# Row normalisation by columns behind the transposes, a deferred inverse in attention, and new gate order in a two-layer diffusion block

## The reference

```
for layer in (0, 1):
    m_l = split(silu(c) @ w_mod[layer] + b_mod[layer], 6)       # latents
    m_c = split(silu(c_ctx) @ w_mod[layer] + b_mod[layer], 6)   # context
    z = concat(rms(xc) * (1 + m_c[1]) + m_c[0], rms(xl) * (1 + m_l[1]) + m_l[0])
    layer 0: p = z @ w_in; half is mixed by an RWKV-7 scan, half by a gated linear
             recurrence (RG-LRU), both ways in time; y @ w_out
    layer 1: differential attention: softmax(s0) @ v - lam * softmax(s1) @ v, rms, y @ w_o
    x = x + m[2] * y
    h = rms(x) * (1 + m[4]) + m[3]
    x = x + m[5] * peer(h)       # 8 heads x 16 experts per token, gathered from a table
```

## Time and profile before

| | |
|---|---|
| median of 3 runs | 3174.97 us (3174.1 to 3178.06) |
| the profiled execution | 3177.49 us, its span 3175.6 us |
| mean granted clock of TensorE | 0.956 |
| PE busy | 2640.8 us (83%) |
| DVE busy | 2108.9 us (66%) |
| POOL busy | 1077.6 us (34%) |
| ACT busy | 679.6 us (21%) |
| HBM read | 928 MB, mean 293 GB/s |

### The profile page before, as it was taken

The page is one execution under the profiler, slowest core; times in us unless marked ns, Lnnn a source line. Parts: engine busy times, 40 slices in busy tenths (PEclk is TensorE's granted clock), DMA queues, the critical chain, the costliest instruction groups (busy, mean ns, idle before and its releaser), DMA issues. The chain is left out here.

```text
span 3175.6 us, 31187 instructions
## 1 busy us (share of the span) xinstructions
PE 2640.8 (83%) x9164; PEld 1303.7 (41%) x9164; DVE 2108.9 (66%) x4866; ACT 679.6 (21%) x1701; POOL 1077.6 (34%) x927
## 2 busy tenths in 40 slices
PE   4996999996899998787777787776987788887777
PEld 2441888883444443222322232223434444432222
DVE  2236334335567777888888888885575677778887
ACT  1025333331221211111111111112024222111111
POOL 0002233222144444444444444441000243344443
PEclk8997999998999999999999999998998899999999
DMA  5224000005499999999999999997422699999998
GB/s 203 80 100 195 1 1 1 1 1 216 168 400 400 398 405 396 421 421 417 416 421 421 420 413 421 420 420 296 169 69 93 255 419 420 420 419 411 421 421 333
DMA packets 137393, 930.65 MB, mean 293 GB/s; under 512 B 16954, under 2 KB 17978, under 8 KB 32330
## 3 DMA queue, kind: packets, MB, share of 16 engines
q0 software_dynamic: 113664, 822.20, 63.2%
q1 hardware_dynamic: 23636, 107.25, 8.9%
HBM read 928.26 MB, written 1.13 MB: 293 GB/s over the span
## 5 line engine op out<-in xcount | busy, mean ns | idle before, releaser
L1469 PE MATMUL psum<-ring,diag 128*128 128x512 f32 x3072 | 1495.7, 622 | 350.6 <-DVE diag L1588 348.7
L1347 POOL DMA_INDIRECT ring<-in_uv,experts x768 | 914.3, 1191 | 1283.8 <-PE psum L1469 1036.2
L1642 DVE CUSTOM_DVE_ANT_0 ring<-ring,hcur 128x1024 f32<-128x1024 f32 x768 | 941.6, 1226 | 303.6 <-DMA ring<-in_uv,experts 276.0
L1469 PEld LDWEIGHTS psum<-ring,diag 128*128 128x128 f32 x3072 | 558.0, 194 | 1200.1 <-DVE diag L1588 726.0
L1377 ACT ACTIVATE gel<-dots 128x1 f32<-128x1 f32 x768 | 148.6, 201 | 1419.3 <-DVE dots L1642 1418.0
L1588 DVE TENSOR_SCALAR diag<-ident,gel,wcur 128x128 f32<-128x128 f32 x768 | 257.6, 345 | 21.9 <-ACT gel L1377 21.9
L1059 DVE COPY_PREDICATED T<-level,psum 128x512 f32<-128x512 uint32 x80 | 58.6, 733 | 173.8 <-PE psum L824 173.8
L344 PE MATMUL psum<-zT,win_ring 128*128 128x512 f32 x368 | 161.4, 599 | 1.4 <-PEq L90 1.4
L1708 PE MATMUL psum<-wqkv_ring,zT 128*128 128x512 f32 x320 | 139.4, 598 | 1.4 <-PEq L90 1.4
L1448 PE MATMUL psum<-yT,w_q 128*128 128x512 f32 (+1 forms) x256 | 120.3, 572 | 2.6 <-issue 2.6
L344 PEld LDWEIGHTS psum<-zT,win_ring 128*128 128x128 f32 x368 | 70.2, 192 | 87.8 <-issue 87.8
(11 more groups left out here) (368 smaller groups left out, 2702.0 us busy)
## 6 DMA issues: line engine op xcount, KB each, us to landing
wmod<-in_w_mod SPq DMA_DIRECT2D x24, 1024.0 KB, 8.8
w_q<-in_w_q SPq DMA_DIRECT2D x36, 512.0 KB, 7.9
wmod<-in_w_mod POOLq DMA_DIRECT2D x16, 1024.0 KB, 5.5
ring<-in_uv,experts POOLq DMA_INDIRECT x768
wqkv_ring<-in_w_qkv SPq DMA_DIRECT2D x6, 2048.0 KB, 10.7
win_ring<-in_w_in SPq DMA_DIRECT2D x23, 512.0 KB, 3.6
wring<-in_w_mod SPq DMA_DIRECT2D x4, 2048.0 KB, 11.7
bc<-modulation_rows SPq DMA_DIRECT2D x14, 512.0 KB, 13.0
```

Source lines behind the costliest of these rows:

```text
L1347: nc.gpsimd.indirect_dma_start(ring[:, s % RING], None, uv, bass.IndirectOffsetOnAxis(ap=experts[:, n, j:j + 1], axis=0)).then_inc(row_in[ ...
L1469: m = nc.tensor.matmul(ps[:, c], diag[:, j % DIAGS], ring[:, j % RING, D + 512 * c:D + 512 * c + 512], start=(first and j == 0), stop=(las ...
L1642: nc.vector.tensor_tensor_reduce(u, u, hcur[:], 1.0, 0.0, ALU.mult, ALU.add, dots[:, j:j + 1]).then_inc(dot_done, 1)
```

## The change

**Layer 0's normalisation moves into `modulation`.** The weight ring becomes four halves of 1 MB, the same tile that `rglru` uses. While slabs arrive, ACT squares x, DVE multiplies x by the inverse root, PE transposes, ACT copies to zT. The rows of shift and scale are no longer written to DRAM; PE turns them to columns, one per partition, and ACT and DVE apply scale and shift to zT in eight pieces of 128x256 each. On PE the transposes stand ahead of the first modulation matmul.

```diff
+                for t in range(TILES):
+                    nc.scalar.activation(z[:, t], X[:, t], ACT.Square, accum_out=ss[:, t:t + 1]).then_inc(ss_done, 1)
...
+                for g in range(2 * TILES):
+                    act.wait_ge(tr_mm, g + 1)
...
+                act.wait_ge(col_done, 1)
+                shift_scale_act(nc, modcol, 0, zT, lambda k, seg: zT[:, k, seg * SEG:(seg + 1) * SEG], range(0, KD, 2), range(2))
...
+                for i in range(HALVES):
+                    if i >= RING:
+                        sp.wait_ge(part_mm, i - RING + 1)
...
+def columns_of(nc, pe, bank, row, ident, row_done):
+    for n in range(FIRST_CHUNKS):
+        if row_done is not None:
+            pe.wait_ge(row_done, n + 1)
+        for c in range(4 * n, 4 * n + 4):
+            m = nc.tensor.transpose(bank[:, 2 * c:2 * c + 2], row[:, c * P:(c + 1) * P], ident[0:2, 0:2])
+    return m
...
+def shift_scale_act(nc, modcol, layer, zT, source, ks, segs, done=None):
+    for seg in segs:
+        for k in ks:
+            nc.scalar.activation(zT[:, k, seg * SEG:(seg + 1) * SEG], source(k, seg), ACT.Identity,
+                                 scale=modcol[:, layer, 1, k, seg:seg + 1], bias=modcol[:, layer, 0, k, seg:seg + 1])
...
+def keep_busy(nc, bank, ident, rhs, count):
+    for _ in range(count):
+        nc.tensor.matmul(bank, ident, rhs, start=True, stop=True)
```

```diff
+                for t in range(2):
+                    nc.scalar.activation(z[:, t], X[:, t], ACT.Square, accum_out=ss[:, t:t + 1]).then_inc(ss_done, 1)
...
+                for seg in range(2):
+                    act.wait_ge(tr_mm, seg + 1)
+                    shift_scale_act(nc, modcol, 1, zT, source, (0, 1, 4, 5), (seg,))
...
+                    nc.vector.tensor_scalar(z[:, t], X[:, t], ss[:, t:t + 1], None, ALU.mult).then_inc(z_done, 1)
+                    if t == 1:
+                        dve.wait_ge(col_mm, 1)
...
+                keep_busy(nc, ps[:, 0], ident[:], X[:, 0, 0:512], 4)
+                pe.wait_ge(row_in, 16)
+                columns_of(nc, pe, ps[:, 7], row, ident, None).then_inc(col_mm, 1)
```

```diff
-        MOD_AT = lambda u: range(u, u + 1)
+        ROOTS_AT = {3: range(0, 4), 5: range(4, 6), 7: range(6, 8)}
+        SCAN_AT = {4: (0,), 5: (1,), 6: (2,), 7: (3, 4)}
...
-                    if u >= 1:
-                        for n in MOD_AT(u - 1):
-                            mod_groups(n)
-                for n in MOD_AT(7):
-                    mod_groups(n)
+                    if u >= 2:
+                        mod_groups(u - 2)
+                mod_groups(6)
+                mod_groups(7)
                 add_groups(len(LRU_CHUNKS) - 1)
+                keep_busy(nc, ps[:, 0], gw[:, 0], xb[:, 0], 8)
...
-                    if u % 4 == 3:
+                    if u in ROOTS_AT:
                         act.wait_ge(v_done, u + 1)
-                        for q in range(u - 3, u + 1):
+                        for q in ROOTS_AT[u]:
                             nc.scalar.activation(vv[:, q], vv[:, q], ACT.Sqrt).then_inc(m_done, 1)
-                    for n in MOD_AT(u):
...
+                    if u >= 2:
+                        copy_part(u - 2)
+                copy_part(6)
+                copy_part(7)
...
-                    if u >= 4:
-                        scan(u - 4)
-                    if u >= 1:
-                        for n in MOD_AT(u - 1):
-                            mod_row(n)
-                for u in range(4, 8):
+                    for q in SCAN_AT.get(u, ()):
+                        scan(q)
+                    if u >= 3:
+                        mod_row(u - 3)
+                for u in range(5, 8):
                     scan(u)
-                    if u == 4:
-                        for n in MOD_AT(7):
-                            mod_row(n)
+                    mod_row(u)
```

```diff
-                    if g >= 4:
-                        late(g - 4)
+                    if g in (4, 6):
+                        late((g - 4) // 2)
...
-                    nc.scalar.activation(sq[:, u % 2], ps[:, OUT, 0:P], ACT.Square, accum_out=ss[:, u % 2, u // 2:u // 2 + 1]).then_inc(sq_done, 1)
+                    nc.scalar.activation(sq[:, u % 2], ps[:, OUT, 0:P], ACT.Square, scale=inv[:, u % 2, 0:1], accum_out=ss[:, u % 2, u // 2:u // 2 + 1]).then_inc(sq_done, 1)
...
-                    tt(o[:, u % 2, u // 2], ps[:, OUT, 0:P], sub_g[:], ALU.mult).then_inc(o_done, 1)
+                    nc.vector.scalar_tensor_tensor(o[:, u % 2, u // 2], ps[:, OUT, 0:P], inv[:, u % 2, 0:1], sub_g[:], ALU.mult, ALU.mult).then_inc(o_done, 1)
...
-                    step(nc.vector.reciprocal(tot[:, b], tot[:, b]))
-                    step(tt(tot[:, b, 1:2], tot[:, b, 1:2], nlam[:], ALU.mult))
-                    step(nc.vector.tensor_scalar(A[:, b], E[:, b, 0], tot[:, b, 0:1], None, ALU.mult))
-                    nc.vector.scalar_tensor_tensor(A[:, b], E[:, b, 1], tot[:, b, 1:2], A[:, b], ALU.mult, ALU.add).then_inc(a_done, 1)
+                    if u >= 2:
+                        dve.wait_ge(o_done, u - 1)
+                    step(nc.vector.reciprocal(inv[:, b], tot[:, b]))
+                    step(nc.vector.tensor_scalar(inv[:, b, 1:2], inv[:, b, 1:2], tot[:, b, 0:1], nlam[:], ALU.mult, ALU.mult))
+                    nc.vector.scalar_tensor_tensor(A[:, b], E[:, b, 1], inv[:, b, 1:2], E[:, b, 0], ALU.mult, ALU.add).then_inc(a_done, 1)
```

More of the change, by code:

```diff
@@ L254, in _ @@
             def _(sp):
-                for seg in segs:
-                    for i, part in enumerate((shift, scale)):
-                        sp.dma_start(bc[:, seg, i], row_of(mod, layer, seg, part)).then_inc(bc_in, 16)
-                if load_next:
-                    load_next(sp)
+                sp.dma_start(row[:], mod[1, :, 0:2 * D]).then_inc(row_in, 16)
+                load_next(sp)
             @block.scalar
             def _(act):
-                for i, t in enumerate(tiles):
-                    if i >= 2:
-                        act.wait_ge(ss_done, i - 1)
-                    nc.scalar.activation(squares[:, i % 2], X[:, t], ACT.Square, accum_out=ss[:, i:i + 1]).then_inc(ss_done, 1)
+                for t in range(2):
+                    nc.scalar.activation(z[:, t], X[:, t], ACT.Square, accum_out=ss[:, t:t + 1]).then_inc(ss_done, 1)
@@ L267, in _ @@
                 act.wait_ge(mean_done, 1)
                 nc.scalar.activation(ss[:], ss[:], ACT.Sqrt).then_inc(std_done, 1)
-                for g in range(2 * nt):
-                    act.wait_ge(tr_done, g + 1)
-                    i, half = g // 2, 4 * (g % 2)
-                    nc.scalar.activation(hT[:, half:half + 4, i * P:(i + 1) * P],
-                                         ps[:, g % 8].rearrange("p (c t) -> p c t", c=4), ACT.Copy).then_inc(ev_done, 1)
+                act.wait_ge(col_done, 1)
@@ L1848, in values, with late @@
                     m.then_inc(pv_mm, 1)
-                def late(n):
-                    if n >= 2:
-                        pe.wait_ge(late_done, n - 1)
-                    nc.tensor.matmul(ps[0:2, 6 + n % 2], ones[:], mod_acc[:, n], start=True, stop=True).then_inc(late_mm, 1)
+                def late(j):
+                    for g in range(GROUPS):
+                        m = nc.tensor.matmul(ps[32 * g:32 * g + 32, 6 + j], ones[:], mod_acc[:, GROUPS * j + g], start=True, stop=True)
+                    m.then_inc(late_mm, 1)
                 pe.wait_ge(ones_done, 1)
```

199 lines of the change are left out of this document (125 added, 74 removed).

## The result

The changed kernel takes 3153.8 us (median of 4 runs, 3150.7 to 3156.1) where the kernel before, on the same chip, took 3176.5. The ratio is 0.9932 (95% interval 0.9920 to 0.9944): faster, by 17.8 to 25.4 us, that is by less than 1%. The forecast was 3144.5, that is 30.5 us less, with a range of 3138 to 3152; the measured time lies outside it. The profiled execution took 3153.75 us, so it stands at the median and needs no correction.

What follows compares the result with a forecast made beforehand. No engine is busy for the whole span, so it was read by phase: -17.2 + 5.7 - 0.5 - 3.8 - 8.2 - 6.5 = -30.5 us, from a median of 3175.0 to 3144.5, range 3138 to 3152.

Steps and rivals of the forecast that it cites:

- part 2: Gates' stage: the new order makes ACT wait for PE ahead of each Tanh; +5.7 us, bounds -4.5 to +11.
- part 6: Attention: -6.5 us, 6 from transposes, 0.5 from the loop; a ring of waits between ACT and DVE keeps its period 3.46.
- Part 1: Opening: first projection matmul at 46.9 us, 17.2 saved; 21 if the ring of four half slabs does not run dry.
- Part 3: Scan phase: fillers fit ahead of the first matmul and release little; -0.5 us, 0 to -2.
- Part 5: Layer 1's normalisation: squares shared by ACT and DVE, next matmul at 2197; -8.2 us, bounds -6.5 to -9.5.
- Part 4: Both output projections: short filler matmuls take the half-clock start into PE's idle time; 1.9 us each, -3.8 together.
- Each unit takes 6.3 us: Gates' stage from unit 3 on: 3.0 us of ACT standing still plus 3.3 from Tanh to the copy's end.
- Last, the filler: End of the gates' stage: eight filler matmuls, queued behind the last sum, start at half clock and end last, at 303.6.
- Rival (a): Gates' stage: the copy does not hold the gates; gates -4.5, sum -41, 3134 us; chance 0.1.
- Rival (b): Attention: the loop shortens with DVE's lighter work; 8 us more saved, 3136 us; chance 0.08.
- Rival (c): Projections and gates: fillers fail to raise the clock; +0.6 for -3.8, gates +10.5, sum -21, 3154 us; chance 0.12.
- Rival (d): Layer 0's projection and scan: added matmuls lower TensorE's granted clock, making the kernel slower than before; chance 0.02.

## Why the prediction was right and wrong

The time came out at 3153.8, outside 3138 to 3152; from this set's 3176.5 for the kernel before, the forecast would have been 3146. Two steps failed: in part 2 the unit of 6.3 us and what ends the stage, in part 6 the period that was to stay at 3.46. In the profile they are 2.8 and 2.5 us of the 6.8 missing; 1.6 more came from a slow TensorE at the end of attention, which no step foresaw. Part 2's 8.5 us lie inside the bounds given for it (-4.5 to +11); attention's loop had none on the side where it gets longer.

**Part 1 held**: 46.96 for a forecast 46.9, and the dry ring with it, shown by the run that fills it. That it fits to 0.1 is luck: kernels with the same opening have 46.8 to 48.5. **Part 3** was -0.4, in a stage that differs by 4 us between kernels with the same code for it, so nothing speaks against it and nothing shows it. **Part 5** was -8.9 for -8.2. **Part 4** was -5.2 for -3.8; 1.7 and 3.0 of it go when the fillers go, so the mechanism is right and the second projection's share was put too low.

**Part 2: mechanism right, two terms wrong.** ACT does stand still ahead of each Tanh, and one move of PE's list removes it. The failed terms: (1) "Each unit takes 6.3 us", built on a wait of 3.0 as at full clock. Here PE had itself been idle for 5.04 us, and the sum and the gates then took 1.86 and 3.36 us for the 1.02 and 1.98 of the next unit; the granted clock was 0.55 in the one and 1.00 in the other:

```profile
239.40:244.60 5.20, 5.13 (x10) 1.31 (x14) 0.00 (x0) 1.30 (x2) 0.00 (x0) 0.55 0.43 173
247.90:251.00 3.10, 2.98 (x10) 0.88 (x14) 2.81 (x4) 0.08 (x2) 0.00 (x0) 1.00 1.00 418
```

The wait I had found makes the engine that is waited for slower. From copy to copy the two units in which PE had been idle for 5.04 and 4.00 us took 8.56 and 7.99 for the 6.3; the one between, with two roots, took 8.79 for 8.7. The last copy that stands on the chain ended 50.05 us into the stage for a forecast 47.4, and DVE 6.2 us later than before for the 3.3 forecast. (2) "Last, the filler": the fillers did end behind DVE, at 290.06, but POOL's issue of the last row, 288.54 + 2.87, holds the next stage just as long, and alone when they are gone. I had moved the last row behind the last scan in my sum and not asked who waits for it. Rival (a) is out: it would have needed ACT's Tanhs to run without waits.

The Trainium skill's rule on table sets ("ScalarE: Activation LUTs", section "Table sets: the hidden batching unit") did speak against this edit, but for another reason. The extra pair of table loads is 2 x 1.28. The first of them, at 253.83, is over at 255.11 and its root starts at 255.13, so nothing stands behind it; the load at 277.10 that the prediction went by can't show this, since ACT then waited 1.53 us for DVE. The kernel with three root batches and PE's gates ahead is 2.0 us longer than the one with two (63.8 and 61.8), and POOL's last issue alone, 2.3 us, would explain that. PE's list took 13.1 of the 15.1 us.

**Part 6: the ring right, its length wrong.** "The period stays at 3.46" took the ring as given and counted only what the change removes from DVE, none of which is on it. What the change adds is on it: the square takes 0.36 with the per-partition scale for 0.27, the output copy 0.35 for 0.29. Together 0.15, and the period is 3.61; with the old scaling it is 3.46 again. Over the first 13 periods that is +2.0 us, where the sum had -0.5 for the loop. A further 1.6 is in the last two (6.59 us for 5.02). It goes with a granted clock of 0.71 for 1.00 there, and it is not the loop's edit: the kernel with the rows first, whose loop is the same, has 4.83 us in one profile, at 1.00, and 6.20 in the other, at 0.77. Whether the change makes this ending more frequent is open; the one trace of the kernel before has the short one. The transposes' part gave 5.9 of the forecast 6 (the last copy ends 10.55 us into the stage, 16.44 before). Rival (b) is out while the ring is closed, and a quarter true once it is open.

**Rival (c)** had the right size (3154) and the wrong reason: the fillers work, as the 1.7 and 3.0 us show. **Rival (d)**: "no row shows a busy stretch slowing down" is no longer so (the dips with the rows first), but they are not this change's: its own profile has none, and they did not turn the sign.

## What to carry to other kernels

When work is taken from one engine, list what the edit adds to the ring that holds the loop before counting what it takes from the engine with the most busy time: here 0.15 us of operands outweighed 0.5 us of work, and exchanging two steps of DVE's list was worth 9.0 us over 13 units. When a step is delayed by a unit, follow it through each in-order list: whether the next unit's matmul stands ahead of or behind the delayed wait decided 13 us. And the last instruction of a phase is not only the end of its own engine: a DMA that waits for it holds the next phase.

## What the runs showed of the hardware

- TensorE's granted clock was 0.86, 0.96 and 0.93 in the mean over three stretches (12, 48 and 24 us) where PE was busy over 93% of the time, in one execution, and 1.00 in another of the same kernel on another chip; the scan stage differed by 7.6 us.
- At the end of attention the granted clock was 0.71 to 0.78 in six profiles and 1.00 in others, and once each way in two executions of one kernel; its last two periods took 6.20 and 4.83 us.
- After 5.04 us of idle time in the midst of a stage PE's next two groups ran at a granted clock of 0.55, about the 1.2 GHz level.
- A per-partition scale added 0.09 us to a 128x128 square on ACT, and a scalar operand 0.06 to a 128x128 product on DVE.
- From POOL's last DMA issue of a phase to its first instruction in the next it was 2.87 or 2.88 us in the three kernels read in which that issue is last; where DVE ended last, POOL went on 1.1 to 1.4 us behind it.
